# First norm's root on ScalarE alone, whole tiles evicted by VectorE, and the mixer's fill in two lumps per pass

## What is computed

```python
def rms_norm(x, g, eps=NORM_EPS):
    xf = x.astype(jnp.float32)
    y = xf * lax.rsqrt(jnp.mean(xf * xf, axis=-1, keepdims=True) + eps)
    return (y * g.astype(jnp.float32)).astype(x.dtype)
...
h = jnp.concatenate([meta, x], axis=1)
h = h + hybrid_mixer(rms_norm(h, norm1_g[l]), w_in[l], ...)
h = h + hierarchical_moe(rms_norm(h, norm2_g[l]), moe_wg[l], ...)
return h[:, N_META:]
```

## Time and profile before

| | us |
|---|---|
| median of 3 runs | 930.11 (929.64 to 930.90) |
| the profiled execution, its own time | 930.29 |
| its span (first to last instruction) | 928.5 |
| TensorE busy with matmuls | 884.8 (95%) |
| VectorE, ScalarE, GpSimd busy | 285.6, 196.6, 100.0 |
| mean granted TensorE clock | 0.986 of full speed |

### The profile page before, as it was taken

How to read it: one execution, slowest core, us unless ns; L and a number is a source line. 1 busy time by engine, 2 the same in 40 slices (tenths; PEclk the granted TensorE clock), 3 DMA queues, 4 the chain that set the end, 5 groups by cost and what they waited for, 6 DMA issues and landing times.

```text
span 928.5 us, 16339 instructions
## 1 busy us (share of the span) xinstructions
PE 884.8 (95%) x6978; PEld 509.1 (55%) x6978; DVE 285.6 (31%) x587; ACT 196.6 (21%) x390; POOL 100.0 (11%) x225
## 2 busy tenths in 40 slices
PE   3999999999998999999999999999999998999995
PEld 2878888877776765445454444444445563333331
DVE  3244810312312321452312244333531143222212
ACT  5134101122016111132302111135002220111100
POOL 7720000000003200002000000000000001221121
PEclk9999999999999999999999999999999989999998
DMA  8212127000000000037121113015555068899972
GB/s 230 59 47 81 56 71 204 2 2 3 2 2 1 2 3 25 24 92 194 46 63 28 45 46 85 8 53 199 171 223 238 23 261 306 310 382 385 385 267 109
DMA packets 76136, 109.77 MB, mean 118 GB/s; under 512 B 16892, under 2 KB 61068, under 8 KB 71969
## 3 DMA queue, kind: packets, MB, share of 16 engines
q1 hardware_dynamic: 71296, 93.22, 29.5%
q0 software_dynamic: 4768, 15.52, 5.8%
HBM read 100.32 MB, written 10.50 MB: 119 GB/s over the span
## 4 chain that ended last, share of the span: by engine, by line
PE 91%; DVE 2%; DMA 2%; ACT 2%; issue 1%; SPq 0%; DVEq 0%; POOL 0%; POOLq 0%; ACTq 0%
PE ps L1489 19%; PE ps L1514 10%; PE ps L1847 9%; PE ps L1466 8%; PE ps L1433 8%; PE ps L1793 6%; PE ps L1754 5%; PE ps L1873 5%; PE ps L1471 4%; PE ps L1669 1%; PE ps L1737 1%; PE ps L1834 1%; PE ps L1711 1%; PE ps L1661 1%; PE ps L1687 1%
## 5 line engine op out<-in xcount | busy, mean ns | idle before, releaser
L1489 PE MATMUL ps<-arena 128*128 128x512 f32 x304 | 142.6, 606 | 0.0
L1489 PEld LDWEIGHTS ps<-arena 128*128 128x128 f32 x304 | 54.7, 191 | 62.8 <-issue 60.9
L1514 PEld LDWEIGHTS ps<-arena 64*64 64x64 f32 x2376 | 73.3, 134 | 23.7 <-issue 13.7
L1847 PE MATMUL ps<-arena 128*32 128x512 f32 x624 | 84.9, 592 | 0.5 <-DVE arena L1292 0.5
L1514 PE MATMUL ps<-arena 64*64 64x64 f32 x2376 | 80.3, 220 | 1.6 <-ACT arena L780 1.3
L1433 PE MATMUL ps<-arena 128*128 128x264 f32 x320 | 74.5, 392 | 0.6 <-PE ps L1433 0.6
L1433 PEld LDWEIGHTS ps<-arena 128*128 128x128 f32 x320 | 61.0, 192 | 13.3 <-issue 1.7
L1466 PE MATMUL ps<-arena,h 128*128 128x264 f32 x256 | 65.5, 397 | 0.5 <-PE ps L1433 0.5
L1793 PE MATMUL ps<-arena 128*128 128x512 f32 x128 | 56.2, 594 | 0.0
L1754 PE MATMUL ps<-yT_all,arena 128*128 128x512 f32 x112 | 51.9, 616 | 2.1 <-DMA arena<-in_w_p_fox 1.9
L1466 PEld LDWEIGHTS ps<-arena,h 128*128 128x128 f32 x256 | 45.9, 188 | 9.5 <-issue 0.8
(11 more groups left out here) (344 smaller groups left out, 1036.2 us busy)
## 6 DMA issues: line engine op xcount, KB each, us to landing
arena<-in_moe_w_down SPq DMA_DIRECT2D x32, 512.0 KB, 14.7
arena<-in_moe_w_gate SPq DMA_DIRECT2D x13, 1024.0 KB, 11.3
arena<-in_moe_w_up SPq DMA_DIRECT2D x13, 1024.0 KB, 15.1
arena<-in_w_in SPq DMA_DIRECT2D x19, 512.0 KB, 3.9
arena<-in_w_in SPq DMA_DIRECT2D x5, 1024.0 KB, 9.6
h<-in_x SPq DMA_DIRECT2D x8, 512.0 KB, 5.1
arena<-in_w_out SPq DMA_DIRECT2D x1, 4096.0 KB, 12.8
h<-in_w_in SPq DMA_DIRECT2D x3, 1024.0 KB, 5.3
```

The lines of the kernel that those rows point to most:

```text
L1489: ins = mm(ps[:, gate_bank(n), :], weights_of_gate(n)[:, c, :], nT[:, c, META:L], start=(c == 0), stop=(c == DC - 1))
L1514: ins = mm(psf[q, 512 * bank + c * CH:512 * bank + (c + 1) * CH], lhs(q, c), rhs(q, c), start=True, stop=True)
L1847: ins = mm(ps[rs, bank, :].rearrange("p (h n) -> p h n", h=2), xgT[:, s, c, rs], w1[ws][:, :, c, :], start=(c == 0), stop=(c == DC - 1))
```

## The change

Four things are changed:

1. **The root.** `eps_c` is set first of all by VectorE, and ScalarE does square, Ln (with scale 1/1024 and bias eps) and Exp in a row (`first_norm`). Tile 0 comes ahead of the meta rows, in the DMAs, on ScalarE, on VectorE and on TensorE, and g1 is loaded ahead of tiles 1 to 3. VectorE waits for g1 behind the scaling of tile 0 and meta.
2. **The evictions.** VectorE takes all eight blocks of tiles 0, 1 and 2 out of PSUM in one instruction each (`chunks_out`). Tile 3 is still shared with ScalarE. No ScalarE eviction stands between the squares.
3. **The masks.** `reset` is built ahead of the level masks, and `consts_ready` is raised there for the first time; the recurrence waits for the second.
4. **The fill.** The two steps behind the second transposes, and the one behind each of the five products, are gone. Five steps stand behind the last transposes (`TURN_FILL`) and nine behind the last product (`INIT_FILL`); the sum per pass is 14 in both kernels, and so is `HEAD_FILL`.

The diff, without the hunk that only renumbers a wait (`consts_ready` from NT + 1 to NT + 2):

```diff
...
 SHIFT_ORDER = (4, 1, 2, 0, 3)
-INIT_FILL = 4
+INIT_FILL = 9
+TURN_FILL = 5
 LEVEL_FILL = 3
...
             for k_ in range(4):
-                pe_order.append((("tr", p_, k_), {1: 2, 3: 3 + 5}.get(k_, 0)))
+                pe_order.append((("tr", p_, k_), TURN_FILL if k_ == 3 else 0))
             pe_order.append((("init", p_), INIT_FILL))
...
         def _(sp):
+            sp.dma_start(h[:, 0, :], x[0:P, :]).then_inc(sem("tile_in0"), 16)
             sp.dma_start(metax[0:META, :], meta).then_inc(sem("meta_in"), 16)
-            for t in range(NT):
+            sp.dma_start(g1c, g1.rearrange("(c p) -> p c", p=P)).then_inc(sem("g1_in"), 16)
+            for t in range(1, NT):
                 sp.dma_start(h[:, t, :], x[t * P:(t + 1) * P, :]).then_inc(sem(f"tile_in{t}"), 16)
-            sp.dma_start(g1c, g1.rearrange("(c p) -> p c", p=P)).then_inc(sem("g1_in"), 16)
...
+            done(g.memset(reset[:], 1.0))
+            done(g.memset(reset[:, 0:L:CH], 0.0), "consts_ready")
             for lv in range(6):
...
                     done(g.tensor_copy(lev_st[q, lv, :], mask_tmp[q, lv, :]))
-            done(g.memset(reset[:], 1.0))
-            done(g.memset(reset[:, 0:L:CH], 0.0))
             done(g.iota(iota_f[:], [[1, P]], base=0, channel_multiplier=0, allow_small_or_imprecise_dtypes=True))
...
             log_exp_tables()
-            act.wait_ge(sem("meta_in"), 16)
-            done(a.activation(tmp_shift[0:META, :, :].rearrange("p a b -> p (a b)")[:, 0:D], metax[0:META, :], ACT.Square,
-                              accum_out=stat[0:META, 4:5]), "ss_ready")
             act.wait_ge(sem("ms_ready"), 1)
-            inverse_root(stat[0:META, 4:5], "rstd_ready")
-
-            def high_chunks_out(t):
-                act.wait_ge(sem("xT_psum"), t + 2)
-                for c in range(T_SPLIT, DC):
-                    o = 1024 * t + c * P
-                    ins = a.activation(nT[:, c, META + t * P:META + (t + 1) * P], psf[:, o:o + P], ACT.Copy, scale=g1c[:, c:c + 1])
-                done(ins, "nT_high")
+
+            def first_norm(ss, dump, src, rows):
+                done(a.activation(dump, src, ACT.Square, accum_out=ss))
+                done(a.activation(ss, ss, ACT.Ln, scale=1.0 / D, bias=eps_c[0:rows]))
+                done(a.activation(ss, ss, ACT.Exp, scale=-0.5), "rstd_ready")
             for t in range(NT):
                 act.wait_ge(sem(f"tile_in{t}"), 16)
-                done(a.activation(xs[:, t, :], h[:, t, :], ACT.Square, accum_out=stat[:, t:t + 1]), "ss_ready")
-                act.wait_ge(sem("ms_ready"), t + 2)
-                inverse_root(stat[:, t:t + 1], "rstd_ready")
+                first_norm(stat[:, t:t + 1], xs[:, t, :], h[:, t, :], P)
                 if t == 0:
-                    act.wait_ge(sem("g1_in"), 16)
-                if t >= 1:
-                    high_chunks_out(t - 1)
-            high_chunks_out(NT - 1)
+                    act.wait_ge(sem("meta_in"), 16)
+                    first_norm(stat[0:META, 4:5], tmp_shift[0:META, :, :].rearrange("p a b -> p (a b)")[:, 0:D], metax[0:META, :], META)
+            act.wait_ge(sem("g1_in"), 16)
+            act.wait_ge(sem("xT_psum"), NT + 1)
+            t = NT - 1
+            for c in range(T_SPLIT, DC):
+                o = 1024 * t + c * P
+                ins = a.activation(nT[:, c, META + t * P:META + (t + 1) * P], psf[:, o:o + P], ACT.Copy, scale=g1c[:, c:c + 1])
+            done(ins, "nT_high")
             act.wait_ge(sem("params_in"), 336)
...
+            done(v.memset(eps_c, EPS), "ms_ready")
             for j in range(SC):
                 done(v.memset(U[:, j, 0:1], 0.0))
-            dve.wait_ge(sem("ss_ready"), 1)
-            done(ts(stat[0:META, 4:5], stat[0:META, 4:5], 1.0 / D, EPS, ALU.mult, ALU.add), "ms_ready")
-            dve.wait_ge(sem("rstd_ready"), 1)
-            done(ts(metax[0:META, :], metax[0:META, :], stat[0:META, 4:5], None, ALU.mult), "xs_ready")
-            dve.wait_ge(sem("g1_in"), 16)
             gain = lambda c1, n: g1c[:, 0:c1].rearrange("p (c a) -> p c a", a=1).broadcast_to([P, c1, n])
-            def low_chunks_out(t):
-                dve.wait_ge(sem("xT_psum"), t + 2)
-                done(tt(nT[:, 0:T_SPLIT, META + t * P:META + (t + 1) * P],
-                        psf[:, 1024 * t:1024 * t + T_SPLIT * P].rearrange("p (c n) -> p c n", c=T_SPLIT), gain(T_SPLIT, P), ALU.mult), "nT_low")
+            def chunks_out(t, c1):
+                dve.wait_ge(sem("xT_psum"), t + 1 if t == 0 else t + 2)
+                done(tt(nT[:, 0:c1, META + t * P:META + (t + 1) * P],
+                        psf[:, 1024 * t:1024 * t + c1 * P].rearrange("p (c n) -> p c n", c=c1), gain(c1, P), ALU.mult), "nT_low")
             for t in range(NT):
-                dve.wait_ge(sem("ss_ready"), t + 2)
-                done(ts(stat[:, t:t + 1], stat[:, t:t + 1], 1.0 / D, EPS, ALU.mult, ALU.add), "ms_ready")
+                dve.wait_ge(sem("rstd_ready"), t + 1 if t == 0 else t + 2)
+                done(ts(xs[:, t, :], h[:, t, :], stat[:, t:t + 1], None, ALU.mult), "xs_ready")
                 if t == 0:
-                    dve.wait_ge(sem("xT_psum"), 1)
+                    dve.wait_ge(sem("rstd_ready"), 2)
+                    done(ts(metax[0:META, :], metax[0:META, :], stat[0:META, 4:5], None, ALU.mult), "xs_ready")
+                    dve.wait_ge(sem("g1_in"), 16)
+                if t >= 1:
+                    chunks_out(t - 1, DC)
+                if t == 1:
+                    dve.wait_ge(sem("xT_psum"), 2)
                     done(tt(nT[:, :, 0:META], ps[:, 7, 0:DC * META].rearrange("p (c n) -> p c n", c=DC), gain(DC, META), ALU.mult), "nT_meta")
-                dve.wait_ge(sem("rstd_ready"), t + 2)
-                done(ts(xs[:, t, :], h[:, t, :], stat[:, t:t + 1], None, ALU.mult), "xs_ready")
-                if t >= 1:
-                    low_chunks_out(t - 1)
-            low_chunks_out(NT - 1)
-            done(v.memset(eps_c, EPS))
+            chunks_out(NT - 1, T_SPLIT)
             dve.wait_ge(sem("params_in"), 336)
...
+            dve.wait_ge(sem("consts_ready"), 2)
             bc = lambda m_: m_.rearrange("p (a t) -> p a t", a=1).broadcast_to([P, NCH, CH])
...
             pe.wait_ge(sem("ident_ready"), 1)
-            pe.wait_ge(sem("xs_ready"), 1)
-            for c in range(DC):
-                ins = tr(ps[:, 7, c * META:(c + 1) * META], metax[0:META, c * P:(c + 1) * P], ident[0:META, 0:META])
-            ins.then_inc(sem("xT_psum"), 1)
             for t in range(NT):
-                pe.wait_ge(sem("xs_ready"), t + 2)
+                pe.wait_ge(sem("xs_ready"), 1 if t == 0 else t + 2)
                 if t == NT - 1:
...
                 ins.then_inc(sem("xT_psum"), 1)
+                if t == 0:
+                    pe.wait_ge(sem("xs_ready"), 2)
+                    for c in range(DC):
+                        ins = tr(ps[:, 7, c * META:(c + 1) * META], metax[0:META, c * P:(c + 1) * P], ident[0:META, 0:META])
+                    ins.then_inc(sem("xT_psum"), 1)
             pe.wait_ge(sem("nT_meta"), 1)
...
                             pe.wait_ge(sem("nT_low"), 2 * hf + 2)
-                            pe.wait_ge(sem("nT_high"), 2 * hf + 2)
+                            if hf == 1:
+                                pe.wait_ge(sem("nT_high"), 1)
                         for c in range(DC):
...
             pe.wait_ge(sem("fill_out"), 2)
+            pe.wait_ge(sem("consts_ready"), 2)
             quads = [slice(0, 64), slice(64, 128)]
...
                     units(6 * (k % 2), cm(z), idq).then_inc(sem("tr_psum"), 1)
-                    if k == 1:
-                        fill_qkv(2)
...
                 ins.then_inc(sem("tr_psum"), 1)
-                fill_qkv(3)
+                fill_qkv(TURN_FILL)
                 for k, (lhs, rhs) in enumerate(((Kt, At), (Kt, Rt), (Bt, At), (Bt, Rt), (At, Bt))):
...
                     units(4 + 2 * (k % 2), cm(lhs), cm(rhs)).then_inc(sem("g_psum"), 1)
-                    fill_qkv(1)
                 fill_qkv(INIT_FILL)
```

2 lines of the change are left out of this document (1 added, 1 removed).

## The result

| | before | after |
|---|---|---|
| median, us | 929.88 (925.28 to 930.90, 4 runs) | 919.41 (917.39 to 922.00, 4 runs) |
| the profiled execution, its own time | 930.29 | 921.35 |
| its span | 928.5 | 919.6 |
| TensorE busy with matmuls | 884.8 | 881.1 |

The ratio is 0.9899, with a 95% interval of 0.9852 to 0.9945: 1.0% faster.

A forecast was written before the change was run, and what follows sets the result against it. TensorE, busy 95% of the span, bounds the kernel, so time is won where it stands still or works worse than it could. Head 6.2 plus recurrence 4.2 is 10.4 off 930.29: 919.9, set at 919.8 us; range 916.8 to 924.8.

The forecast's parts named there:

- A: The forecast case: both the head's and the recurrence's gains arrive, total 917.5 to 922 us; chance 0.68.
- 6.2 and 4.2: The two gains in us: 6.2 for the head (bounds 3 to 6.8), 4.2 for the recurrence's fill.
- The transposes' 5.9: Head: tile 3's transposes start at 15.5 instead of 21.43, 5.9 us earlier, if everything behind moves along.
- Late next, the parameters: Before the low-rank product: parameters still land at 31.2, leaving 1.4 us; the head can give at most about 6.8 us.
- The clock: Head: half clock cost the projection 1.3 us; full earlier saves up to 2.1 more, the parameters letting 0.9 through.
- Rival E: Full clock from tile 2 on, parameters bounding the head: 6.8 instead of 6.2, total 919.2; chance 0.2 of A's 0.68.
- Masks: GpSimd: building reset earlier costs nothing; level masks come a memset later, needed only behind the whole projection.
- The recurrence's 15 x 0.33 = 5.0: Recurrence: five fewer returns from fill to groups in each of three passes, 0.33 us each, save 5.0 us.
- The stalls' 0.8: Recurrence: product groups three and five wait 0.09 each, perhaps paying 0.15 again; 0.6 to 1.5 us lost, 0.8 taken.
- Rival B: Head gives half: parameters or tiles 3 us later, or longer half clock; head 3, recurrence 2 to 4, 923 to 925; chance 0.22.
- Rival C: Slower: each recurrence group waits for the eviction ahead, 1.0 us each, 18 us in all, total 937; chance 0.03.
- Rival D: Nothing arrives: a later stage with its own pace takes the gain back, 929 to 931; chance 0.04.

The follow-up runs named there:

- e11: The changed kernel run again unaltered, on the same chip as e10: 918.03 us, against 928.31 for the kernel before, ratio 0.9887.
- e3: The changed kernel with chunk 0 no longer waiting for all 21 parameters, mu raising a semaphore of its own: 917.62 us, ratio 0.9892.
- e8: The kernel of e3 with 26 unused transposes of the identity ahead of tile 0: 915.61 us, ratio 0.9865.
- e9: The changed kernel with 26 unused transposes of the identity ahead of tile 0, chunk 0 still behind all parameters: 920.45 us, one execution.
- e6: The changed kernel with the mask reset built last again, behind the level masks: 917.45 us, one execution.
- e7: The changed kernel with the five fill steps split, two behind the second transposes, three behind the last: 920.71 us, one execution.
- e1: The kernel before with only the fill changed, in two lumps per pass: 922.28 us, ratio 0.9944.
- e2: The changed kernel with the fill as it was before, so the head's parts alone: 923.07 us, ratio 0.9949.
- e10: The kernel of e8 with 3, 6, 9 and 6 more idle transposes behind tile 0, meta, tile 1 and tile 2: 914.05 us, ratio 0.9850.

## Why the prediction was right

The forecast (A, 919.8) holds: 919.4, and both mechanisms are the ones forecast. That the two agree to 0.4 us is luck: runs of one kernel spread over 5 us here. The two terms were 6.2 and 4.2; the traces give 5.6 and 4.9, so the head gave 0.6 less and the fill 0.7 more than forecast, and 0.4 each way stood in no term (below).

- **The transposes' 5.9.** They came 5.5 earlier, with two errors that met. Tile 0 landed at 5.42 where I took 4.6: it took 4.6 us from its issue at 0.78, and 4.6 - 0.78 would have been 3.8. VectorE took 1.23 us for 1024 columns where I allowed 1.38, and 0.75 to 0.80 for a scaling where I took 0.9. The last tile stood at about 15.9, inside 15 to 16 by a hair (16.02 in e11, just outside).
- **Late next, the parameters.** Right in kind, and the term that was mis-sized. I let them land at 31.2 and gave TensorE 1.4 us in hand. They landed at 32.5, and TensorE's wait of 1.5 us took most of what the clock had given (next point). "Their issue does not move" is the step that failed: the last was issued at 29.33 instead of 28.07. With it failed "VectorE is ready for chunk 0 at 34.63 whatever happens": it was ready at 35.91, 1.28 later, as the parameters were, and the Tanh ended at 40.98 instead of 39.7. The head was therefore capped at about 5.6, not 6.8. e3 and e8 show the cap and what lay behind it: with the waits gone 40.6, with the clock as well 39.5.
- **The clock.** Rival E's condition came true in part: the projection ran at full clock from its start in both profiles of the changed kernel (14.42 us for 64 matmuls, here and in e11), but tile 2 was still at half in both, and tile 3 was mostly so here (16 transposes in 3.74 us). In half of the profiles with this head the projection began at half. Its gain over the forecast, 6.8 instead of 6.2, didn't come, because the parameters took it. The Trainium skill (TensorE: Matmul & The Clock Gate, What's actually happening) says that activity releases the throttle; the 1.09 us of a tile behind idle transposes in e9 agrees. The head of 6.8 us that I had worked out from its rule did not come; the 0.6 us by which the total would differ are less than the medians can tell.
- **Masks.** Nothing, as said; e6 shows it.
- **The recurrence's 15 x 0.33 = 5.0.** Right: e7 measures 0.33 and 0.34 for one return. The Trainium skill (TensorEngine Tiling, Key Properties) says that a change of tiling mode drains TensorE; a price of 0.33 us agrees with that, though no run separates a drain from other costs of a return.
- **The stalls' 0.8.** Oversized. The two waits of 0.09 per pass came as computed (0.10 each). What I added for "a waiting group may also pay its 0.15 again" did not come, so they cost 0.2 per pass and 0.6 in all.
- **Not in the sum.** Waits that TensorE had before went. One is the fill's: 0.28 us in pass 0 for VectorE's predicated copy (L1053), which is gone in e1 and still there in e2. I had looked for the cover of that copy in pass 1 alone, where no wait stood. With it the fill gives 1.90 + 1.53 + 1.51 = 4.9. The sum 5.0 + 0.28 - 0.6 is 4.7; the last 0.2 or 0.3 have no name. The other wait is 0.47 us in pass 2's scan (L1066), whose first round is 0.38 shorter (1.59 to 1.21 us). It goes in e2 and stays in e1, so it came with the head, for a reason that no run shows, and the 0.36 us more ahead of L1658 cancel it.
- **Rival B**, half a head, was wrong about the amount, though its reason (parameters later) came in part: 1.3 us later, not 3. **Rival C** is refuted: VectorE's 0.76 us fits into a group of 1.05, and the step costs 0.10 where it had to cost 0.73. The Trainium skill (TensorEngine Tiling, PSUM Bottleneck) warns that emptying PSUM may become the limit of packed matmuls (the prediction left out the "may"); here it doesn't, by the 0.29 and 0.39 us that VectorE stood idle between its evictions. **Rival D** is refuted by the table: all later stages keep the shift, but for the clock's 1.7 us and the 0.36 ahead of L1658.

In the profiled pair the forecast would have missed by 1.5 us (921.35 against 919.9), because of the extra stretch at half clock. Two of the four runs had a higher mean clock (0.993 and 0.994 against 0.988) and took 917.4 and 917.5 us.

## What to carry to other kernels

Interleaved filler work has a price per return that no list of waits shows; read it from starts of rows (one in a row, two in a row), and put the filler into as few lumps as the evictions allow, here 0.33 us for each of 15. Before costing a removed wait, list what lands or ends within 2 us behind it, and treat its date as a measured value that can move: here two limits, a DMA and the clock, stood within 1 us of each other, and taking away one alone bought 0.4 us or nothing, while both together gave 1.5. When nothing else bounds the start, idle matmuls in TensorE's pauses can hold its clock without delaying the real ones: in e10 the last tile started at 15.90, in the changed kernel at 15.9 to 16.0. And don't credit an edit with a median before its trace has been compared stage by stage: of the 4.0 us between e10 and e11, 2.1 at most are the head's.
